# Expert outputs of a PEER layer: gathered value rows against products with the whole table

## What is computed

```python
q = (xb @ wq).reshape(PEER_BLOCK, PEER_HEADS, 2, PEER_DKEY // 2)
s = jnp.einsum('thpd,pkd->thpk', q, subkeys)      # 2 x 128 key scores per head
s1, i1 = lax.top_k(s[:, :, 0], 16)
s2, i2 = lax.top_k(s[:, :, 1], 16)
cand = s1[..., :, None] + s2[..., None, :]        # 256 candidates, top 16 of them
idx = i1 * 128 + i2                               # of the 16 chosen
g = jax.nn.softmax(top_s, axis=-1)
act = jax.nn.gelu(jnp.einsum('thkd,td->thk', u_tab[idx], xb))
out = jnp.einsum('thkd,thk->td', v_tab[idx], g * act)
```

## Time and profile before

| | us |
|---|---|
| median of 3 runs | 2052.54 |
| lowest and highest | 2040.8, 2053.34 |
| span of the profiled execution | 2046.0 |
| mixer, in that span | 0 to 715 |
| expert stage | 715 to 2046 |

### The profile page before, as it was taken

How to read it: one execution, slowest core, us unless ns; L and a number is a source line. 1 busy time by engine, 2 the same in 40 slices (tenths; PEclk the granted TensorE clock), 3 DMA queues, 4 the chain that set the end, 5 groups by cost and what they waited for, 6 DMA issues and landing times.

```text
span 2046.0 us, 20838 instructions
## 1 busy us (share of the span) xinstructions
PE 1616.0 (79%) x5461; PEld 764.0 (37%) x5461; DVE 1207.7 (59%) x3129; ACT 476.3 (23%) x1217; POOL 1134.0 (55%) x1168
## 2 busy tenths in 40 slices
PE   6979989983767457768888888788878789599966
PEld 1524546451126113223433344333433344255422
DVE  2222355867766701116767766677667689679972
ACT  1221313130101021212223222222222223223321
POOL 3000021322873555777777667767777677577773
PEclk8989999996775679998999989899999899899988
DMA  8795676896995599999999999999999999799995
GB/s 319 254 364 207 215 263 218 305 337 135 355 385 179 198 401 404 392 416 394 400 420 420 400 368 418 419 373 420 420 401 391 388 403 419 308 412 417 414 372 226
DMA packets 237575, 713.43 MB, mean 349 GB/s; under 512 B 23102, under 2 KB 49056, under 8 KB 237457
## 3 DMA queue, kind: packets, MB, share of 16 engines
q0 software_dynamic: 156672, 570.49, 71.2%
q1 hardware_dynamic: 80488, 140.73, 19.4%
q10 hardware_dynamic: 312, 1.07, 0.2%
HBM read 704.42 MB, written 8.25 MB: 348 GB/s over the span
## 4 chain that ended last, share of the span: by engine, by line
PE 19%; DMA 14%; DVE 12%; issue 7%; POOL 7%; ACT 5%; DVEq 0%; POOLq 0%; ACTq 0%
PE ps_y L2316 13%; DVE u_rows L2095 6%; DMA v_rows<-in_peer_v_dram,expert_idx_ring 5%; DMA v_rows<-in_peer_v_dram,tile_idx 5%; PE ps_r L2290 4%; POOL u_rows L1890 3%; DMA u_rows<-in_peer_u_dram,expert_idx_ring 3%; POOL v_rows L1896 2%; POOL v_rows L1904 2%; ACT wt_diag L1987 2%; PE ps_y L2331 2%; DMA v_rows<-in_peer_v_dram,sample_idx 1%; DVE key_scores_w L2106 1%; ACT L2002 1%; ACT L2033 1%
## 5 line engine op out<-in xcount | busy, mean ns | idle before, releaser
L2316 PE MATMUL ps_y<-v_rows,wt_diag 128*128 128x512 f32 x1664 | 796.9, 621 | 146.6 <-DMA v_rows<-in_peer_v_dram,expert_idx_ring 65.2
L2316 PEld LDWEIGHTS ps_y<-v_rows,wt_diag 128*128 128x128 f32 x1664 | 311.4, 197 | 571.1 <-issue 547.5
L1890 POOL DMA_INDIRECT u_rows<-in_peer_u_dram,expert_idx_ring x384 | 368.2, 959 | 164.7 <-issue 90.3
L2095 DVE CUSTOM_DVE_ANT_0 u_rows<-u_rows,ps_y 128x1024 f32<-128x1024 f32 x360 | 420.4, 1218 | 64.1 <-DMA u_rows<-in_peer_u_dram,expert_idx_ring 58.1
L1896 POOL DMA_INDIRECT v_rows<-in_peer_v_dram,expert_idx_ring x384 | 366.7, 955 | 120.2 <-issue 99.3
L341 POOL DMA_INDIRECT low_rows<-in_peer_u_dram,tile_idx x128 | 174.7, 1364 | 214.7 <-DVE tile_dots L333 148.5
L607 PE MATMUL ps_z<-w_stream,hT 128*128 128x512 f32 (+5 forms) x560 | 249.0, 602 | 36.9 <-DMA w_stream<-in_w_in_dram 19.7
L2331 PE MATMUL ps_y<-v_rows,wt_diag 64*64 64x512 f32 x1024 | 135.1, 645 | 57.4 <-DMA v_rows<-in_peer_v_dram,tile_idx 50.8
L333 DVE CUSTOM_DVE_ANT_0 low_rows<-low_rows,tile_rows 128x1024 f32<-128x1024 f32 x128 | 152.9, 1232 | 44.1 <-DMA low_rows<-in_peer_u_dram,tile_idx 31.9
L607 PEld LDWEIGHTS ps_z<-w_stream,hT 128*128 128x128 f32 (+1 forms) x560 | 100.9, 185 | 163.9 <-issue 132.6
L1904 POOL DMA_INDIRECT v_rows<-in_peer_v_dram,tile_idx x128 | 122.1, 954 | 71.8 <-PE ps_y L2331 44.6
(11 more groups left out here) (434 smaller groups left out, 1628.3 us busy)
## 6 DMA issues: line engine op xcount, KB each, us to landing
w_stream<-in_w_in_dram SPq DMA_DIRECT2D x25, 2048.0 KB, 12.8
w_stream<-in_ada_w_dram SPq DMA_DIRECT2D x12, 2048.0 KB, 12.8
w_stream<-in_peer_wq_dram SPq DMA_DIRECT2D x8, 1024.0 KB, 8.5
wq<-in_peer_wq_dram SPq DMA_DIRECT2D x4, 2048.0 KB, 42.2
w_stream<-in_w_in_dram SPq DMA_DIRECT2D x5, 1568.0 KB, 8.5
w_stream<-in_w_in_dram SPq DMA_DIRECT2D x5, 1536.0 KB, 17.5
u_rows<-in_peer_u_dram,expert_idx_ring POOLq DMA_INDIRECT x384, 7.4
v_rows<-in_peer_v_dram,expert_idx_ring POOLq DMA_INDIRECT x384, 7.9
```

Of the source, the lines that this page charges most:

```text
L1890: g.indirect_dma_start(u_rows[:, j, :], None, U, bass.IndirectOffsetOnAxis(where[:, j:j + 1], 0))\
L2095: v.tensor_tensor_reduce(u_rows[:, j, :], u_rows[:, j, :], row[:, :], 1.0, 0.0, ALU.mult, ALU.add, dots[:, par, j:j + 1]).then_inc(s["u_us ...
L2316: mm = nc.tensor.matmul(ps_y[:, c * 512:(c + 1) * 512], diag[:, par, j, :], v_rows[:, j, c * 512:(c + 1) * 512], start=(first and j == 0), ...
```

## The change

Routing, u gathers and dots stay; the v side of tiles 1 to 3 and of the samples becomes dense. An expert's index is i1 * 128 + i2. For a fixed i2 the 128 rows i1 of the v table are a slab, [128, 1024], read by one direct DMA with a pitch of 128 rows (512 KB) per partition. For a tile the output is the sum over i2 of W[i2] transposed times slab, where W[i2] is [128 i1, 128 tokens] and holds a token's weight at the experts it chose.

- Weight blocks: a token's 128 weights, i1 and i2 are transposed to columns (`columns_t`, `columns_out`). Four tokens a group, DVE compares the i1 and i2 columns with 0..127 (`compare`, 1,024 elements), ACT scales the i2 part by the weights (`weigh`, 4 instructions), PE multiplies the two one-hot matrices per token ([i1 x slot] times [slot x i2], `build`), and ACT copies the result into the big buffer `region` (`weights_out`). 32 groups a tile, 8 for the samples: 104.
- Pass 1 streams the 128 slabs and multiplies tiles 1 and 2 (4 products a slab); from i2 = 90 it also builds tile 3's weights. Pass 2 streams them again for tile 3 (2 products a slab) and the samples (per four slabs 8 products with 32 columns of weights). A slab waits for a free buffer: 4 in pass 1, 8 in pass 2.
- Queries and scores of all heads are computed at the start, for 416 tokens at once (`head`), written to DRAM (`score_rows`) and read back per head. DVE's loop over 26 rounds G (8 heads for each of 3 tiles, 2 for the samples) takes 16 dots each, with `keys` and `pairs` of G + 2 and some comparisons between; a comparison follows slots 177, 179, .. 239 (tile 1), 262 to 293 (tile 2), and from 390 on (tile 3).
- Tile 0 keeps gathered v rows, but with full 128 x 128 diagonals; 40 of its gathers are issued at the start, then one after every second u gather.
- Finishing of all tiles moves behind pass 1, its DMAs to POOL's queue.

The diff, cut to its core:

```diff
+ST = NT
+SGR = 2
 QS = P // NS
-SG = PH * TOPK // QS // NB
-LAST_ROWS = 8
-LAST_KEYS = {**{k: (LT - 1) * PH + k + 1 for k in range(2, 7)}, **{k: LT * PH + k - LAST_ROWS for k in range(LAST_ROWS, GPT)}}
-LAST_PAIRS = {k + 1: H for k, H in LAST_KEYS.items()}
-RINGH = 4
-V0_HEADS = (4, 6)
-HP = P // 2
+HEADS = NH + SGR
+SLOTS = HEADS * TOPK
+V0_EARLY = 5
+HALF = P // 2
+TG = 4
+TILE_GROUPS = P // TG
+W_BASE = {1: 0, 2: TILE_GROUPS, 3: 2 * TILE_GROUPS, ST: 3 * TILE_GROUPS}
+W_COUNT = {1: TILE_GROUPS, 2: TILE_GROUPS, 3: TILE_GROUPS, ST: NS // TG}
+BANK_BASE = {T: W_BASE[T] + T - 1 for T in W_BASE}
+W3_FROM = 90
...
+DOT_GROUPS = {}
+for _n in range(TILE_GROUPS):
+    DOT_GROUPS.setdefault((NH - PH - 5) * TOPK + 2 * _n + 1, []).append(_n)
+    DOT_GROUPS.setdefault(2 * PH * TOPK + 6 + _n, []).append(TILE_GROUPS + _n)
+    DOT_GROUPS.setdefault(3 * PH * TOPK + 6 + _n, []).append(2 * TILE_GROUPS + _n)
+LATE_GROUPS = [_n for _k in sorted(DOT_GROUPS) if _k >= SLOTS for _n in DOT_GROUPS[_k]]
+S_DOT_GROUPS = TILE_GROUPS - len(LATE_GROUPS)
...
+        region = sb("expert_weights", [P, 2, PK, P])
+        R0, R1 = region[:, 0].rearrange("p e t -> p (e t)"), region[:, 1].rearrange("p e t -> p (e t)")
+        v_ring, u_rows = sb("v_ring", [P, 4, D]), sb("u_rows", [P, NB, D])
+        spare = sb("spare_rows", [P, 2 * D])
+        onehot = sb("pair_onehots", [P, 2, 2, TG, PK])
...
+        W = {1: region[:, 1], 2: region[:, 0],
+             ST: u_rows[:, 0:4, :].rearrange("p j d -> p (j d)").rearrange("p (e t) -> p e t", t=NS)}
+        low_halves = region[:, :, 0:HALF, :]
+        tail_v = [v_ring[:, j, :] for j in range(4)] + [u_rows[:, j, :] for j in range(4, NB)]
...
+        def slab(n):
+            if n < PK:
+                return v_ring[:, n % 4, :], e_in[n % 4], n // 4 + 1
+            m = n - PK
+            return tail_v[m % 8], e_in[m % 8], m // 8 + 1 + (PK // 4 if m % 8 < 4 else 0)
...
+                for h in range(PH):
+                    sp.wait_ge(s["staged"], h + 1)
+                    out = s[f"st_out{h % 2}"]
+                    sp.dma_start(sc_dram[0:LT * P, h, :].rearrange("(t p) k -> p t k", p=P), staged[:, h % 2, 0:LT, :])\
+                        .then_inc(out, 16)
+                    sp.dma_start(sc_dram[LT * P:, h, :], staged[0:NS, h % 2, LT, :]).then_inc(out, 16)
+                    sp.wait_ge(out, 32 * (h // 2 + 1))
+                    if h >= 2:
+                        sp.wait_ge(s["keys_done"], h - 1)
+                    sp.dma_start(sc[:, h % 2].rearrange("p k n -> p (k n)"), sc_dram[0:P, h, :]).then_inc(s[f"sc_in{h % 2}"], 16)
+                sp.wait_ge(s["sc_full"], 2 * PH)
+                for n in range(2 * PK):
+                    dst, landed, _ = slab(n)
+                    m = n - PK
+                    if m < 0:
+                        if n >= 4:
+                            sp.wait_ge(s["passed"], n - 3)
+                    elif m < 4:
+                        sp.wait_ge(s["passed"], PK - 3 + m)
+                    elif m < 8:
+                        sp.wait_ge(s["u_used"], SLOTS)
+                    else:
+                        sp.wait_ge(s["passed"], PK + (m - 8) // 4 * 4 + 4)
+                    sp.dma_start(dst, I["peer_v"][0].rearrange("(a b) d -> a b d", b=PK)[:, n % PK, :]).then_inc(landed, 16)
...
+                for k in range(NB):
+                    v0_gather(k)
...
+                for k in range(NB, V0_EARLY * NB):
+                    v0_gather(k)
+                pool.wait_ge(s["h_normed"], NT)
+                for G in range(HEADS):
+                    pool.wait_ge(s["routed"], G + 1)
+                    if PH <= G + 2 < HEADS:
+                        load_scores(G + 2)
+                    if G == 12:
+                        for q in range(QS):
+                            g.dma_start(h_smp[q * NS:(q + 1) * NS, :], hrow[ST]).then_inc(s["hs_in"], 16)
+                    first = (V0_EARLY + G) * NB
+                    for r in range(TOPK):
+                        u_gather(G, r)
+                        if r % 2 and first < P:
+                            v0_gather(first + r // 2)
...
+                def weigh(T, n):
+                    act.wait_ge(s["oh_cmp"], n + 1)
+                    for t in range(TG):
+                        col = (n - W_BASE[T]) * TG + t
+                        last = a(onehot[:, n % 2, 1, t, :], onehot[:, n % 2, 1, t, :], ACT.Copy, scale=tT[:, 0, col:col + 1])
+                    last.then_inc(s["oh_w"], 1)
...
+                    if T == 3:
+                        a(low_halves[:, :, :, t0:t0 + TG], src.rearrange("p (h e) t -> p h e t", h=2), ACT.Copy).then_inc(s["w_out"], 1)
+                    else:
+                        a(W[T][:, :, t0:t0 + TG], src, ACT.Copy).then_inc(s["w_out"], 1)
...
+                columns_out(1)
+                build(1, 0, 24)
+                gates_exp(2)
+                build(1, 24, 32)
+                dots_gelu(2)
+                columns_out(2)
+                act.wait_ge(s["hs_in"], 16 * QS)
+                act.wait_ge(s["h_placed"], 3)
+                build(2, 32, 64)
+                gates_exp(3)
+                gates_exp(ST)
+                dots_gelu(3)
+                columns_out(3)
+                act.wait_ge(s["passed"], HALF)
+                build(3, 64, 64 + S_DOT_GROUPS)
+                dots_gelu(ST)
+                build(3, 64 + S_DOT_GROUPS, 96)
+                columns_out(ST)
+                build(ST, 96, 96 + W_COUNT[ST])
+                act.wait_ge(s["passed"], PK)
+                y_copies(2, y_sb[2])
+                y_copies(1, y_sb[1])
+                for k in range(3):
+                    root(k)
+                root(3)
+                act.wait_ge(s["passed"], 2 * PK)
+                y_copies(ST, ys_sb)
+                root(4, NS)
...
+                def compare(n):
+                    T = max(t for t in W_BASE if W_BASE[t] <= n)
+                    dve.wait_ge(s["w_out"], BANK_BASE[T] + 1)
+                    if n >= 2:
+                        dve.wait_ge(s["w_full"], bank_use(n - 2) + 1)
+                    t0 = (n - W_BASE[T]) * TG
+                    v.tensor_tensor(onehot[:, n % 2], iota[:, :].unsqueeze(1).unsqueeze(1).broadcast_to([P, 2, TG, PK]),
+                                    repeat_last(tT[:, 1:3, t0:t0 + TG], PK), ALU.is_equal).then_inc(s["oh_cmp"], 1)
...
+                for G in range(2):
+                    keys(G)
+                    pairs(G)
+                for G in range(HEADS):
+                    T = tile_of(G)
+                    if G and T != tile_of(G - 1):
+                        place_rows(T)
+                    if T == 2:
+                        dve.wait_ge(s["diag_ready"], columns(G).stop)
+                    for r in range(TOPK):
+                        take_dot(G, r)
+                        if r == 3 and G and T != tile_of(G - 1):
+                            weights(T - 1)
+                        if r == 3 and G + 2 < HEADS:
+                            keys(G + 2)
+                        if r == 11 and G + 2 < HEADS:
+                            pairs(G + 2)
+                        if r == 11 and (G % PH == PH - 1 or G == HEADS - 1):
+                            normalise(T)
+                        for n in DOT_GROUPS.get(G * TOPK + r, ()):
+                            compare(n)
+                for n in LATE_GROUPS[:1]:
+                    compare(n)
+                weights(ST)
+                for n in LATE_GROUPS[1:]:
+                    compare(n)
+                for n in range(96, 96 + W_COUNT[ST]):
+                    compare(n)
...
-                def sums(i, par, slots, first=False):
-                    for j in slots:
-                        hold(pe, s["diag_ready"], i * NB + (j + 1) + GPT * NB)
-                        hold(pe, v_in[j], i * 16 + 16 + GPT * 16)
-                        for c in range(2):
-                            mm = nc.tensor.matmul(ps_y[:, c * 512:(c + 1) * 512], diag[:, par, j, :],
-                                                  v_rows[:, j, c * 512:(c + 1) * 512], start=(first and j == 0), stop=False,
-                                                  skip_group_check=True)
-                        mm.then_inc(s["v_used"], 1)
...
+                def build(n):
+                    use = bank_use(n)
+                    pe.wait_ge(s["oh_w"], n + 1)
+                    pe.wait_ge(s["w_out"], use - 1)
+                    for t in range(TG):
+                        mm = nc.tensor.matmul(ps_w[use % 2][:, t * PK:(t + 1) * PK], onehot[:, n % 2, 0, t, :],
+                                              onehot[:, n % 2, 1, t, :], start=True, stop=True)
+                    mm.then_inc(s["w_full"], 1)
+                def products(n, weights, of):
+                    rows, landed, count = slab(n)
+                    pe.wait_ge(landed, 16 * count)
+                    for c in range(2):
```

(76 more changed lines are left out.)

780 lines of the change are left out of this document (331 added, 449 removed).

## The result

| | before | after |
|---|---|---|
| median, us | 2050.93 | 2295.88 |
| lowest and highest | 2040.8, 2053.34 | 2294.42, 2303.09 |
| span of the profiled execution | 2046.0 | 2293.1 |
| moved by DMA, MB | 713 | 636 |

The ratio on record is 1.1206, with a 95% interval of 1.1168 to 1.1244 (the two medians by themselves give 1.119): 12% slower, 247 us in span, although 77 MB less are moved. The forecast was 2,294 us.

What follows compares the result with a forecast made beforehand. DMA and POOL's gather issue were taken to bound the stage behind the mixer; summed along time, dots to 1,477 us, two PE-bound passes to 2,271, tail to 2,288, plus 6.5 gave 2,294 us, 12% slower, range 2,225 to 2,385.

Steps and rivals of the forecast that it cites:

- outside the span: Time added from profiled span to median, taken from the kernel before: 6.5 us, giving 2,294 us.
- Step 1: Start to first round of gathers: POOL's tile 0 gather waits for group 4 on PE; ends at 835 us.
- Step 2: Rounds 0 to 10: 24 gathers a round at 1.244 us, 29.9 us on POOL; slot 176 at 1,174 us.
- Step 3: Slots 176 to 293: DVE sets the pace, 28.0 us a round, plus comparisons, columns and chain; ends at 1,477 us.
- my bounds: Cost of 64 new DVE comparisons before pass 1: between 73 and 97 us, taken as 77.
- Step 4: Pass 1: 439 us of PE products plus building tile 3's weight blocks, 38 us and 2; ends at 1,956 us.
- Steps 5 and 6: Between passes, sample weights 24 us, PE standing; then pass 2, 9.1 us per four slabs, 291 us, to 2,271.
- rival (d): Pass 2: sample products do not overlap, 8 x 0.857 in place of 1.92 us, +158: 2,452 us; chance 0.03.
- (c): Both passes: products cheaper, one 0.43 us instruction each, so faster or equal: 2,001 us; chance 0.04.
- Rival (a): Slab loads: 512 KB pitch halves the rate to 208 GB/s, pass 2 becomes 323 us: 2,331 us; chance 0.18.
- Rival (b): Before pass 1: dots come earlier, start -25, rounds at DVE's pace -20, first columns -10: 2,239 us; chance 0.13.
- Step 7: Tail after the last products: DVE finishes tile 3 (6 us) before the samples; 17 us, end at 2,288 us.

Runs made afterwards that it cites:

- the one with late slabs: Changed kernel, but SP's first slab load of pass 1 waits until 176 dots are taken: 2295.76 us, ratio 1.1197 to the kernel before.
- the run with four early groups: Changed kernel, but four instead of five groups of tile 0 rows gathered before the rounds: 2351.59 us, ratio 1.1448 to the kernel before.

## Why the prediction was right, step by step

Right was what carries the sum: dots first, then two passes in which PE is the bound at 0.857 us a product. That the total fits within 2 us is luck in part: the steps are off by 4 to 20 us each, with both signs. Of the signs named beforehand one was missed by a little: the DMA share in pass 2 is 0.62, not below 0.6.

| step | forecast end | measured end | step's error | why |
|---|---|---|---|---|
| 1, round 0 | 835 | 854.0 | +19 | start of PE's groups |
| 2, slot 176 | 1,174 | 1,212.8 | +20 | bytes of others, rate |
| 3, pass 1 starts | 1,477 | 1,495.5 | -20 | waits that are not there |
| 4, pass 1 over | 1,956 | 1,964.2 | -10 | builds cheaper |
| 5, sample weights | 1,980 | 1,983.6 | -5 | |
| 6, pass 2 over | 2,271 | 2,269.0 | -6 | change of shape cheaper |
| 7, tail | 2,288 | 2,293.1 | +7 | POOL's store |
| outside the span | 2,294.5 | 2,295.9 | -4 | |

**Step 1.** I let PE take tile 0's groups as rows arrive. The first group starts at 739.3, behind a wait of 9 us for ACT, which squares rows ahead of the copy that PE needs (the row above); ACT in turn waits 14 us in three parts for those rows to land. Two groups and the transposes between them then take 38 us, of which I had counted the 32 of the groups. The rest of the step was right: group 4 starts 73.0 us after head 0, forecast 73. Part of an error at this place is scatter that the mixer brings along: its last long block on PE starts at 672.6 us in the changed kernel and at 677.3 in the one with late slabs, 4.7 of the 5.8 us between their first groups. POOL's timeline in the changed kernel shows the wait that step 1 named:

```profile
838.31 0.94 POOL L1940 DMA_INDIRECT u_rows<-in_peer_u_dram,tile_idx_b  x1 [0.30 <-issue]
852.77 0.93 POOL L1930 DMA_INDIRECT expert_weights<-in_peer_v_dram,tile_idx  x1 [13.51 <-PE bank L2327]
854.00 0.94 POOL L1940 DMA_INDIRECT u_rows<-in_peer_u_dram,tile_idx_b  x1 [0.31 <-issue]
```

**Step 2.** The stretch moved 145.7 MB at 406 GB/s. 264 gathers are 138.4 MB, 341 us at that rate; the other 7.3 MB are 18 us. I priced a gather by POOL's cadence, 1.244 us or 421 GB/s, although the row by stretch gave 399: the cadence is what POOL can do, the rate what the DMA engines gave. And I left out who else moves bytes, 128 to 416 KB of score rows per head and the first four slabs, 2.1 MB, which SP loads as soon as it is through with the scores, 480 us before they are needed. Scores and slabs make some 5.7 of the 7.3 MB; what the rest is stays open.

**Step 3.** DVE's pace was right: 278.3 us from slot 176 to the last comparison, of which 64 comparisons at 1.14 us start to start are 73, the low end of my bounds (I took 77); the remaining 205 are the 207 of dots and routing. The 13 us for first columns and row copies are not there: the first comparison comes at 1,215.7, behind no wait. The chain behind the last comparison took 4.4, not 6.

**Step 4.** 128 turns are 439 us; measured are 468.7, so weights cost 30 in place of 40. A build of 8 instructions keeps PE for 0.89 us start to start, 28.5 in all; its 1.16 us in the timeline holds the tail of the last. That the dots behind slot 390 wait and are hidden was right: DVE stands 119 us before the comparison at 1,805.7, and PE has no gap.

```profile
1805.68 1.23 DVE L2228 TENSOR_TENSOR pair_onehots<-iota_f,pair_columns 128x1024 f32<-128x1024 f32 x1 [119.26 <-ACT pair_columns L2055]
```

**Steps 5 and 6.** Timeline of PE in pass 2 of the changed kernel:

```profile
1983.61 7.03 PE L2395 MATMUL token_rows<-v_ring,expert_weights 128*128 128x512 f32 x16
1990.58 1.92 PE L2445 MATMUL bank<-v_ring,u_rows 128*32 128x512 f32 x16
1992.43 7.13 PE L2395 MATMUL token_rows<-u_rows,expert_weights 128*128 128x512 f32 x16
...
2001.35 7.13 PE L2395 MATMUL token_rows<-v_ring,expert_weights 128*128 128x512 f32 x16
```

Sample weights took 19.5 us, 5 less than ACT's pace had given. Pass 2 shows the same 7.03 and 1.92 as in the earlier trace rows, and from the second four slabs on a turn takes 8.92 us start to start (1,992.43 to 2,001.35), where 9.1 had been summed: over 6.86 and 1.92 the two changes of shape add 0.14 us, not 0.3. So rival (d) fell (it wanted 6.9 for the second row), and (c) with it. The Trainium skill, "TensorE: Matmul & The Clock Gate", section "Back-to-back issue gap", gives 131 ns for 512 columns as a sustained rate; 16 instructions in 7.03 us are 0.44 us each, so it does not hold for these fp32 products.

**Rival (a)**, slabs slow for their pitch, fell by three runs: consecutive rows changed nothing, 306 GB/s came without a wait, and without cover the pitch cost 3 to 4 us of 175. The figure of the Trainium skill, "DMA: Bandwidth & Descriptors", section on latency and other measured facts, 207 GB/s at a pitch of 512 KB, is given for copies between HBM tensors with 16 KB to a partition; these loads, 4 KB to a partition from HBM to SBUF, ran at 379 GB/s at that pitch.

**Rival (b)**, earlier dots, fell too, and the run with four early groups shows that it could not be had by earlier gathers alone: once the gathers come early, the scores hold the first dots.

**Step 7.** The store that moved to POOL's queue costs 9.3 us where SP's took 2.3. The forecast named the move but priced the store as before.
